# Fourteen units of neighbourhood attention: probabilities turned by one DMA transpose each, weighed three steps later, outputs scaled behind the exponentials

## The reference, cut to what matters

```
s_loc = einsum('bwhd,biwjhd->bhwij', qr, kwin) * ATTN_SCALE + bias
s_ctx = einsum('bwhd,bchd->bhwc', qr, kc) * ATTN_SCALE
p = softmax(concatenate([s_loc, s_ctx], axis=-1), axis=-1)
return einsum('bhwij,biwjhd->bwhd', p_loc, vwin) + einsum('bhwc,bchd->bwhd', p_ctx, vc)
```

## Time and profile before

| what | value |
|---|---|
| median of 3 runs | 1243.13 us (1242.36 to 1243.44) |
| the profiled execution | 1242.15 us |
| its span, first to last instruction | 1240.4 us |
| PE, DVE, ACT, POOL busy | 98%, 79%, 52%, 32% of the span |
| granted PE clock | 1.00 throughout |
| steps 1 to 31 of the neighbourhood units | 278 to 373 us |

### The profile page before, as it was taken

How to read it: one execution, slowest core, us unless ns; L and a number is a source line. 1 busy time by engine, 2 the same in 40 slices (tenths; PEclk the granted TensorE clock), 3 DMA queues, 4 the chain that set the end, 5 groups by cost and what they waited for, 6 DMA issues and landing times.

```text
span 1240.4 us, 22508 instructions
## 1 busy us (share of the span) xinstructions
PE 1220.8 (98%) x7981; PEld 661.0 (53%) x7981; DVE 982.1 (79%) x1597; ACT 641.5 (52%) x1213; POOL 397.9 (32%) x385
## 2 busy tenths in 40 slices
PE   8999999999999999999999999999999999999998
PEld 1564656556665666664454455554554554444444
DVE  3879998676879999963489888888888885767587
ACT  2642234546679999952155554455545543412325
POOL 0000000114678988840320443445554320000001
PEclk9999999999999999999999999999999999999999
DMA  9728723256410131021300333222223317997953
GB/s 362 278 88 320 257 83 136 81 114 134 141 44 11 35 138 36 2 86 51 119 34 2 102 103 101 84 92 69 77 85 101 101 40 265 351 349 234 373 194 136
DMA packets 125122, 167.74 MB, mean 135 GB/s; under 512 B 22640, under 2 KB 84080, under 8 KB 123632
## 3 DMA queue, kind: packets, MB, share of 16 engines
q1 hardware_dynamic: 125040, 166.65, 40.5%
HBM read 138.57 MB, written 22.55 MB: 130 GB/s over the span
## 4 chain that ended last, share of the span: by engine, by line
PE 68%; DVE 4%; ACT 2%; issue 2%; POOL 1%; DMA 1%; another core or an unknown queue 0%; SPq 0%; POOLq 0%; ACTq 0%; DVEq 0%
PE PS L1380 65%; PE PS L1709 1%; DMA arena<-weight_sum_rows 1%; DVE arena L3498 1%; DVE arena L3501 1%; PE PS L1455 1%; ACT arena L2583 1%; ACT PS L2313 1%; DVE arena L3061 0%; POOL arena L1224 0%; ACT arena L2313 0%; ACT arena L2308 0%; DVE arena L3085 0%; DMA arena<-arena 0%; DVE arena L3040 0%
## 5 line engine op out<-in xcount | busy, mean ns | idle before, releaser
L1380 PE MATMUL PS<-arena 128*128 128x512 f16 (+9 forms) x7485 | 1184.8, 320 | 12.5 <-DMA arena<-in_w_mod 5.7
L1380 PEld LDWEIGHTS PS<-arena 128*128 128x128 f16 (+3 forms) x7485 | 616.1, 100 | 556.5 <-issue 33.8
L3177 DVE SCALAR_TENSOR_TENSOR arena<-arena 128x512 f16<-128x512 f32 x128 | 114.4, 900 | 29.0 <-ACT arena L2405 28.1
L2405 ACT ACTIVATE arena<-arena 128x512 f16<-128x512 f32 x120 | 75.4, 630 | 98.8 <-PE PS L1380 98.8
L2535 ACT ACTIVATE arena<-arena 128x512 f16<-128x512 f32 x77 | 48.2, 629 | 123.4 <-DVE arena L3398 74.6
L3061 DVE TENSOR_REDUCE arena<-PS 128x1 f32<-128x512 f32 (+1 forms) x160 | 106.8, 681 | 2.6 <-PE PS L1380 2.6
L1374 POOL TENSOR_TENSOR arena<-arena 128x1 f32<-128x1 f32 x8 | 4.7, 597 | 230.8 <-DVE arena L3565 226.6
L2308 ACT ACTIVATE arena<-PS 128x512 f16<-128x512 f32 x125 | 75.1, 601 | 2.5 <-PE PS L1380 1.5
L1224 POOL TENSOR_TENSOR arena<-arena 128x512 f16<-128x512 f32 x64 | 74.0, 1157 | 6.9 <-ACT arena L2313 4.3
L3234 DVE TENSOR_TENSOR arena<-PS,arena 128x256 f32<-128x256 f32 (+1 forms) x100 | 55.2, 553 | 24.9 <-PE PS L1380 24.5
L3413 DVE SCALAR_TENSOR_TENSOR arena<-arena 128x512 f16<-128x512 f32 x77 | 52.5, 687 | 19.9 <-ACT arena L2535 19.9
(11 more groups left out here) (225 smaller groups left out, 1291.5 us busy)
## 6 DMA issues: line engine op xcount, KB each, us to landing
arena<-in_w_ffn_out SPq DMA_DIRECT2D x121, 256.0 KB, 4.9
arena<-in_w_mod SPq DMA_DIRECT2D x23, 1024.0 KB, 7.7
arena<-in_w_ffn_in SPq DMA_DIRECT2D x88, 256.0 KB, 3.0
left_operands<-arena SPq DMA_DIRECT2D x43, 256.0 KB, 2.9
arena<-in_w_in SPq DMA_DIRECT2D x9, 1024.0 KB, 5.7
arena<-left_operands SPq DMA_DIRECT2D x3, 2816.0 KB, 11.6
arena<-lay_bias SPq DMA_DIRECT2D x12, 512.0 KB, 3.9
arena<-in_x SPq DMA_DIRECT2D x2, 2048.0 KB, 14.3
```

Source lines behind the costliest of these rows:

```text
L1380: return pe.matmul(out, lhsT, rhs, start=start, stop=stop, skip_group_check=True)
L2405: act.activation(block_split(p, b)[:, 0], weight_block(p, b, first), ACT.Copy, scale=WS).then_inc(blk_hi, 1)
L3177: dve.scalar_tensor_tensor(dst[:, 1], src, WS, dst[:, 0], ALU.mult, ALU.subtract).then_inc(blk_lo, 1)
```

## The change

For 14 of the 32 units, the odd ones from 3 to 29 (`by_dma`), the order of "turn" and "split" is exchanged. ACT writes the exponentials back into the score bank in PSUM, then makes the high f16 half of all 640 from there (`hi_p`, one instruction), DVE makes the low half (one instruction over 640), and both halves, 128 x 1280 f16, lie in one buffer `Phl` (in the place of the odd `Pb`). SP then issues one DMA transpose of `Phl` into the odd `PT`. PE's five transposes of such a unit fall away, and its `weigh` moves from step u + 2 to step u + 3, an even step, ahead of the `weigh` of the even unit after it; the last one, of unit 29, stands at the end of step 31. `scaled` moves as well: in even steps ACT does two of them behind the exponentials, in odd steps none.

New waits: `hi_p(u)` waits until the DMA of unit u - 2 has landed (one `Phl`), `exponentials(31)` until that of unit 29 has (it writes where `Phl` lies), SP's transpose waits for `low_p(u)` and for `weigh(u - 2)`, and `weigh(u)` waits for the landing. `scores(u + 2)` waits for the one `low_p(u)`. The tile `shifts` moves to another place in SBUF.

```
+        self.by_dma = v % 2 == 1 and 1 < v < HN * NT - 1
+        Phl = f16(105.5, 2, 5 * P)
+        PT = [f16(o, 2 * 5, P) for o in (28, 100)]
+            def turn_p(u):                                          # SP
+                sp.wait_ge(pt_lo, u.halves())
+                sp.wait_ge(o_mm, u.v - 1)
+                sp.dma_start_transpose(PT[1], flat(Phl)).then_inc(pt_in, 16)
             for k in range(NNA):                                    # SP
                 if k in pieces:
                     load_bias(pieces[k])
+                if k and Unit(k - 1).by_dma:
+                    turn_p(Unit(k - 1))
                 if k % 4 == 2 and k > 2:
                     turn_qk(GROUP0[0] + k // 4 - 1)
...
-                copied(u, 1)                                        # PE, weigh
+                if u.by_dma:
+                    pe.wait_ge(pt_in, u.landed())
+                else:
+                    copied(u, 1)
...
-                weigh(Unit(k - 2))                                  # PE, step k
-                turn_p(Unit(k - 1))
+                if Unit(k - 3).by_dma:
+                    weigh(Unit(k - 3))
+                if not Unit(k - 2).by_dma:
+                    weigh(Unit(k - 2))
+                if not Unit(k - 1).by_dma:
+                    turn_p(Unit(k - 1))
...
+                if k == NNA - 1:
+                    weigh(Unit(k - 2))
...
+                if u.v == NNA - 1:                                  # ACT, exponentials
+                    act.wait_ge(pt_in, u.ahead(-2).landed())
...
+            def hi_p(u):
+                if u.v > 3:
+                    act.wait_ge(pt_in, u.ahead(-2).landed())
+                act.wait_ge(s_exp, u.v + 1)
+                act.activation(Phl[:, 0], PSf[:, u.scores_at:u.scores_at + 5 * P], ACT.Copy, scale=PSC).then_inc(pt_hi, 1)
...
-                if k > 2:                                           # ACT, step k
+                if k == 3:
                     scaled(Unit(k - 2))
-                copy_p(Unit(k - 1))
+                if not Unit(k - 1).by_dma:
+                    copy_p(Unit(k - 1))
                 exponentials(Unit(k))
+                if Unit(k).by_dma:
+                    hi_p(Unit(k))
+                elif k > 2:
+                    if Unit(k - 3).by_dma:
+                        scaled(Unit(k - 3))
+                    scaled(Unit(k - 2))
...
+                if u.by_dma:                                        # DVE, low_p
+                    dve.wait_ge(pt_hi, u.halves())
+                    dve.scalar_tensor_tensor(Phl[:, 1], PSf[:, u.scores_at:u.scores_at + 5 * P], PSC, Phl[:, 0],
+                                             ALU.mult, ALU.subtract).then_inc(pt_lo, 1)
+                    return
...
                 if k < NNA:                                         # DVE, step k
                     maximum(Unit(k))
+                if Unit(k - 1).by_dma:
+                    low_p(Unit(k - 1))
```

More of the change, by code:

```diff
@@ L312, in __init__, with halves, landed @@
         self.scores_at = 1024 * self.par
+        self.by_dma = v % 2 == 1 and 1 < v < HN * NT - 1
     def turned(self, bank):
-        return 2 * self.v + bank + 1
+        return sum(2 for v in range(self.v) if not Unit(v).by_dma) + bank + 1
+    def halves(self, bank=0):
+        return sum(1 if Unit(v).by_dma else 2 for v in range(self.v)) + bank + 1
+    def landed(self):
+        return 16 + 16 * (self.v // 2)
     def turned_at(self, bank):
@@ L383, in n_low @@
             return self.g * len(POOL_TILES) + sum(i <= self.i for i in POOL_TILES)
-        return 2 * HN * NT + self.g * (NKT - len(POOL_TILES)) + sum(i <= self.i and i not in POOL_TILES for i in range(NKT))
+        return Unit(HN * NT).halves() - 1 + self.g * (NKT - len(POOL_TILES)) + sum(i <= self.i and i not in POOL_TILES for i in range(NKT))
 class Chain:
@@ L1677, in copied @@
             def copied(u, bank):
-                pe.wait_ge(pt_lo, u.turned(bank))
+                pe.wait_ge(pt_lo, u.halves(0 if u.by_dma else bank))
             def scores(u):
@@ L1724, in weigh @@
                     for part, vp in ((0, 0), (1, 0), (0, 1)):
-                        ins = mm(PS[:, 6 + u.par, 0:HD], PT[u.par][part][:, i], v[:, vp],
+                        ins = mm(PS[:, 6 + u.par, 0:HD], PT[u.par][:, 5 * part + i], v[:, vp],
                                  i == 0 and part + vp == 0, i == 4 and vp == 1)
@@ L2273, in exponentials @@
                 act.wait_ge(s_max, n_scored(u.v))
-                act.activation(flat(Pb[u.par]), PSf[:, u.scores_at:u.scores_at + 5 * P], ACT.Exp,
-                               scale=-1.0, bias=nmax[:, u.par:u.par + 1], accum_out=esum[:, u.v % 4:u.v % 4 + 1])\
-                    .then_inc(s_exp, 1)
+                ps = PSf[:, u.scores_at:u.scores_at + 5 * P]
+                if u.v == NNA - 1:
+                    act.wait_ge(pt_in, u.ahead(-2).landed())
+                act.activation(ps if u.by_dma else flat(Pb[u.par]), ps, ACT.Exp, scale=-1.0,
+                               bias=nmax[:, u.par:u.par + 1], accum_out=esum[:, u.v % 4:u.v % 4 + 1]).then_inc(s_exp, 1)
+            def hi_p(u):
[3 more added lines that the diff above has]
+                act.activation(Phl[:, 0], PSf[:, u.scores_at:u.scores_at + 5 * P], ACT.Copy, scale=PSC).then_inc(pt_hi, 1)
             def copy_p(u):
@@ L2284, in copy_p @@
                     o = u.turned_at(b)
-                    act.activation(flat(PT[u.par][0][:, t.start:t.stop]), PSf[:, o:o + len(t) * P],
+                    act.activation(flat(PT[u.par][:, t.start:t.stop]), PSf[:, o:o + len(t) * P],
                                    ACT.Copy, scale=PSC).then_inc(pt_hi, 1)
@@ L3035, in low_p @@
             def low_p(u):
+                if u.by_dma:
[3 more added lines that the diff above has]
+                    return
                 for b, t in enumerate(u.banks):
[L3038 removed]
+                    dve.wait_ge(pt_hi, u.halves(b))
                     o = u.turned_at(b)
[L3040 to L3041 removed]
+                    dve.scalar_tensor_tensor(flat(PT[u.par][:, 5 + t.start:5 + t.stop]), PSf[:, o:o + len(t) * P], PSC,
+                                             flat(PT[u.par][:, t.start:t.stop]), ALU.mult, ALU.subtract)\
                         .then_inc(pt_lo, 1)
@@ L3137, in _ @@
                     chunk_maximum(Step(NKT + 1))
-                low_p(Unit(k - 1))
+                if not Unit(k - 1).by_dma:
+                    low_p(Unit(k - 1))
                 inverse_sum(Unit(k - 1))
```

6 lines of the change are left out of this document (2 added, 4 removed).

## The result

| | before | changed |
|---|---|---|
| median | 1241.93 us (6 runs, 1240.01 to 1243.44) | 1247.11 us (6 runs, 1246.42 to 1249.48) |
| ratio to before | | 1.0042 [1.0032, 1.0052] |
| profiled execution, span | 1242.15, 1240.4 us | 1247.56, 1245.5 us |
| maximum(3) to maximum(31) | 85.90 us | 90.13 us |

The kernel is slower, by 5.2 us. The time lies within the range, on the side of rival B. One execution of experiment 3 took 3308.06 us; its ratio is formed without it.

The account below looks back on a forecast made before the run. PE was taken to bound the neighbourhood units' stage, with DVE next and bounding odd steps after the change. 4.1 us saved less 0.8 at the end gave 3.3, so 1239.8 us; range 1235.6 to 1247.6.

Parts of the forecast that it names:

- rival B: Slower: late DMA landings set the pace; 5.8 us costs 1.95, four such give 1247.6 us; chance 0.22.
- the landing: DMA transposes of 1280 columns in the unit stage: 3.3 us from issue, bounds 2.4 and 6.3.
- landings up to 3.85 cost nothing: Slack before `weigh` and the next `hi_p`: about 0.55 us more is free; each 0.1 beyond costs about 0.1.
- the steady steps: Steps 8 to 27: PE bounds even steps, DVE odd; four take 11.37 against 11.88 us, 2.55 saved.
- issued near 289: `turn_p(3)`, the transpose of unit 3, named as likeliest victim of a late landing.
- the 5.8 us of the earlier trace: One query transpose in the kernel before landed after 5.8 us instead of 3.0.
- rival A: The whole saving arrives, as `low_p` doesn't bound odd steps: 8.1 - 0.8 = 7.3, 1235.8 us; 0.10 including the page's figure.
- Steps 4 to 7: No chunk, no second weighing in step 4, no DVE operation in step 5: 10.45 against 11.49 us, 1.04 saved.
- ACT's spare time: Odd steps' `hi_p` hidden with 0.7 us to spare; even steps leave ACT half empty.
- Stand ahead of the query transpose, the bias load and the weight load: SP's queue: `turn_p` precedes these transfers of the same turn, which are wanted steps later.
- The end: `weigh(29)` and `exponentials(31)` wait for unit 29's landing: 0.6 to 0.9 us later, taken as 0.8.
- The sum: 4.1 us saved in the steps, less 0.8 at the end: 3.3 us less, median 1239.8 us.

Follow-up runs that it names:

- experiment 3: Changed kernel with DMA transposes only from unit 9 on (11 units), stores of the gates in their old place: 1241.14 us, 0.9998 of before.
- experiment 2: Kernel before, with the stores to `gates` moved behind SP's loads of the output weights: 1242.11 us, 1.0010 of before.
- experiment 1: Changed kernel, with the stores to `gates` moved behind SP's loads of the output weights: 1240.55 us, 0.9996 of before.
- experiment 4: Changed kernel with unit 3 alone transposed by DMA, the 13 others turned by PE as before: 1247.67 us, 1.0053 of before.
- experiment 6: Changed kernel with the gates' stores in their old place but in 32-byte pieces from another, dense tile: 1240.45 us, 0.9987 of before.
- experiment 7: Changed kernel with the 4-byte stores of the gates issued in SP's turn 20, ahead of unit 19's transpose: 1249.53 us, 1.0060 of before.
- experiment 10: Changed kernel with late gate stores, SP loads behind `turn_p`, unit 29 by PE; plus `low_p` ahead of DVE's other operation in odd steps: 1245.96 us, 1.0027.
- experiment 11: Changed kernel with late gate stores, and on SP the unit's transpose ahead of the bias load: 1239.08 us, 0.9978 of before.
- experiment 15: Repeat, on another chip, of the changed kernel with late gate stores and transpose ahead of the bias load: 1239.78 us, 0.9984 of before.
- experiment 13: Changed kernel with late gate stores and transpose ahead of bias load; plus ACT's query cast moved behind step 30's exponentials and outputs: 1242.73 us, 0.9998.
- experiment 5: Changed kernel with only the destination order of the gates' stores changed; packets stayed at 4 bytes: 1248.63 us, 1.0049 of before.

## Why the prediction was wrong, step by step

- **The step that failed is the landing**: "I take 3.3", for all fourteen. Thirteen landed between 3.3 and 5.2 us, unit 3 after 9.2, and PE waited 6.11 us for it. The allowance beside it ("landings up to 3.85 cost nothing") was about right in the steady steps: landings of 4.25 and 4.29 lengthened their steps by 0.3 to 0.4. This is rival B with the victim that it named ("issued near 289"), given 0.22. B was priced with the 5.8 us of the earlier trace rows as if landings were drawn at random. I did not look at what stood ahead of it in the trace: the stores to `gates`, issued at 284.3 there, whose packets ran at about 288.5 to 289.6. That they are the cause of this 5.8 is likely but not shown: it became 3.69 without them (experiment 2), but 4.04 with them (experiment 3). The change puts a transpose that PE waits for at 288.97, right behind them. Experiments 1, 4, 6 and 7 show it: without the stores, or with 32-byte pieces, it is gone; one unit alone brings it; it goes where the stores go.
- **A missing term**: the clock behind a long wait. The wait of 6.11 us came with 6.83 us at 1.2 GHz. Step 6 is 11.49 us against 3.37 in experiment 1: 8.1 us, of which 5.8 are more waiting and some 2.3 the clock.
- **Right: the steady steps**, with the forecast in brackets. Even steps 2.72 and 2.93 (2.72, 2.94), odd ones 2.91 (2.91) and 2.71 (2.80). `low_p` over 640 took 0.82 us (0.84), `hi_p` 0.70 (0.71). DVE bounds the odd steps (experiment 10), and rival A is out.
- **Steps 4 to 7** were forecast at 10.45; undisturbed (experiment 1) they take 11.14. Step 6 is 3.37 instead of 2.72, by the same cast of the query path that waits for POOL ahead of the exponentials (0.68 us). I had called ACT's spare time enough, and had left POOL out of the chain. Nor does the 3.85 hold there: by the prediction's own numbers `weigh(3)` is due 2.40 + 2.42 + 0.55 = 5.37 us behind the scores of step 4 and the landing comes at 5.7, and in experiment 1 PE does wait, 0.29 us.
- **Landings of 4.25 to 5.16 us**, at units 13, 15 and 21, lengthen steps 16, 18 and 24 by 0.3 to 1.1 us each, about 2 us in all. "Stand ahead of the query transpose, the bias load and the weight load" was wrong for the bias load: it stands ahead of `turn_p`, and swapping the two is worth 1 to 1.5 us of the stage (experiments 1, 11, 15).
- **The end**: 0.8 us were forecast behind the scores of step 31, by the wait for unit 29. PE's wait is there (1.08 us), but the time from `maximum(31)` to the transposes of unit 31 is what it was (2.99, 3.00). What is lost lies in step 30: 4.17 us instead of the 2.94 forecast, in ACT's queue (experiment 13). That the sizes are near each other is luck.
- **The sum.** Forecast for the stage and its end: -3.3. Measured: +4.2 in the stage and +0.9 behind it, which is the span's +5.1. With the stores moved, the stage is 3.5 shorter than in the kernel before, of which 1.9 is that kernel's own stall, and 1.56 the change. For steps 4 to 30 the forecast was 4.1. The late landings (2.0), step 30 (1.2) and steps 4 to 7 (0.7) more than cover the difference of 2.5; the odd steps of 2.71 and some long steps of the kernel before (9, 25 and 26) work the other way.
- The Trainium skill's rule (DMA: Bandwidth & Descriptors, Rules for kernel authors) that a transpose next to ordinary DMAs needs nothing stands there as one of correctness. Read as one of time it doesn't hold here: with the two small stores ahead a landing is 9.2 us, without them 3.4.

Open: why two small stores hold up the packets behind them for some 8 us after their own; only that they do is shown. Also what the 0.9 us behind `maximum(31)` are: the time from there to the end is 870.3 us before and 871.2 after. In the stretch where the moved stores cost time the two are alike (54.9, 55.0); the difference appears in the last 240 us, where experiment 6, with its stores in the old place too, takes 1.8 more than before.

## What to carry to other kernels

Before a transfer is put where an engine waits for it, read what the DMA engines do at that time: here a window with a share near 1 and 26 GB/s held packets of 4 bytes and what they had held up, and the transpose issued into it was late by 6 us. Moving such stores moves their hold-up; cutting them into larger pieces removed it (experiment 6). An outlier of a duration in the trace may have a cause with a place: look for it before pricing the rival as a chance per instance. Count a long stall of PE with the time at the low clock behind it.

## What the runs showed of the hardware

- Two stores of 4 KB in 4-byte pieces land after 12.7 to 13.7 us (the changed kernel, experiments 4 and 7); in 32-byte pieces after 4.8 and 4.9. A DMA transpose of 1280 columns behind the first takes 9.2 to 12.0 us, behind the second 3.4. Three loads of 1024 KB behind the first land after 16.7 us (median) instead of 10.3 (experiment 2).
- A source that steps over every second f32 was moved in packets of 4 bytes in both orders of the destination that were run (experiment 5).
- Waits of PE of 6.11 us (the changed kernel), 8.10 (experiment 7) and 8.51 (experiment 5) each came with a stretch at the lower clock, 0.50: of 6.83, 10.24 and 6.83 us. The longest wait did not bring the longest stretch.
- DMA transposes within SBUF landed after 2.4 us (512 columns), 3.0 (1024) and 3.3 (1280) at the least.
